# Forgetting attention in key tiles: value products of two tiles in one block, products for the row maxima in the other gap

## The reference

```python
log_f = jax.nn.log_sigmoid((f_logit + b_f).astype(jnp.float32))
Ft = jnp.cumsum(log_f, axis=1).transpose(0, 2, 1)
...
    s = jnp.einsum("bqhd,bkhd->bhqk", qi, k, preferred_element_type=jnp.float32) * scale
    s = s + Fi[..., :, None] - Ft[:, :, None, :]
    ...
    s = jnp.where(kpos[None, :] <= qpos[:, None], s, -jnp.inf)
    p = jax.nn.softmax(s, axis=-1)
    return jnp.einsum("bhqk,bkhd->bqhd", p.astype(v.dtype), v)
```

## Time and profile before

| | |
|---|---|
| median of 3 runs | 3053.46 us |
| span of the profiled execution | 3053.4 us |
| mean granted PE clock over the span | 0.978 |
| PE busy over the span | 2901.2 us, 95% |
| DVE, ACT, POOL busy | 1441.2 us, 1079.7 us, 1064.3 us |
| this attention, layer 1 | from about 1054 to 1292 us of the span |
| this attention, layer 2 | from about 2581 to 2817 us |

### The profile page before, as it was taken

How to read it: one execution, slowest core, us unless ns; L and a number is a source line. 1 busy time by engine, 2 the same in 40 slices (tenths; PEclk the granted TensorE clock), 3 DMA queues, 4 the chain that set the end, 5 groups by cost and what they waited for, 6 DMA issues and landing times. The chain is left out here.

```text
span 3053.4 us, 68189 instructions
## 1 busy us (share of the span) xinstructions
PE 2901.2 (95%) x26644; PEld 2137.6 (70%) x26644; DVE 1441.2 (47%) x2152; ACT 1079.7 (35%) x2188; POOL 1064.3 (35%) x998
## 2 busy tenths in 40 slices
PE   7999989999999899989989999899999998998899
PEld 6867877777777644467768678677777776444677
DVE  5117743323233387767461177432233323877674
ACT  5004433333333234633150044333333332346331
POOL 5101113355555523632151011233555555236221
PEclk9999999999999899999999999999999998999999
DMA  5225543344444341266342255433444443512663
GB/s 159 76 71 166 162 128 95 109 128 131 128 129 128 115 150 40 84 196 205 113 157 76 75 161 161 131 97 109 127 128 132 129 124 115 150 40 84 195 205 114
DMA packets 440642, 383.21 MB, mean 126 GB/s; under 512 B 130696, under 2 KB 369544, under 8 KB 440328
## 3 DMA queue, kind: packets, MB, share of 16 engines
q1 hardware_dynamic: 369576, 345.06, 37.1%
q10 hardware_dynamic: 70752, 33.85, 4.2%
HBM read 239.62 MB, written 139.23 MB: 124 GB/s over the span
## 5 line engine op out<-in xcount | busy, mean ns | idle before, releaser
L147 PE MATMUL ch_acc<-h_hi,ch_w_hi 128*128 128x512 f32 (+1 forms) x2032 | 813.6, 400 | 25.0 <-PEq L144 25.0
L153 PE MATMUL ch_acc<-h_hi,ch_w_lo 128*128 128x512 f32 (+1 forms) x2032 | 821.5, 404 | 0.0
L151 PE MATMUL ch_acc<-h_lo,ch_w_hi 128*128 128x512 f32 (+1 forms) x2032 | 817.7, 402 | 0.0
L147 PEld LDWEIGHTS ch_acc<-h_hi,ch_w_hi 128*128 128x128 f32 (+1 forms) x2032 | 377.6, 186 | 113.0 <-issue 29.1
L151 PEld LDWEIGHTS ch_acc<-h_lo,ch_w_hi 128*128 128x128 f32 (+1 forms) x2032 | 377.1, 186 | 95.9 <-issue 9.8
L153 PEld LDWEIGHTS ch_acc<-h_hi,ch_w_lo 128*128 128x128 f32 (+1 forms) x2032 | 376.9, 185 | 88.0 <-issue 0.3
L115 POOL TENSOR_TENSOR ch_w_lo<-ch_raw,ch_w_hi 128x1024 fp32r<-128x1024 f32 (+1 forms) x62 | 149.8, 2416 | 641.2 <-POOLq L114 641.2
L1814 ACT ACTIVATE fx_prob<-fx_ST 128x512 f32<-128x512 f32 (+3 forms) x320 | 153.9, 531 | 189.6 <-PE fx_ST L1661 95.9
L2069 PE MATMUL so_acc<-ea_wo_hi,so_m_hi 128*128 128x512 f32 x512 | 209.6, 409 | 7.5 <-DVEq L2174 3.8
L2070 PE MATMUL so_acc<-ea_wo_hi,so_m_lo 128*128 128x512 f32 x512 | 204.2, 399 | 0.0
L2071 PE MATMUL so_acc<-ea_wo_lo,so_m_hi 128*128 128x512 f32 x512 | 204.2, 399 | 0.0
(11 more groups left out here) (286 smaller groups left out, 4812.5 us busy)
## 6 DMA issues: line engine op xcount, KB each, us to landing
projT<-ch_stage SPq DMA_DIRECT2D x248, 256.0 KB
ch_raw<-w_in ACTq DMA_DIRECT2D x62, 512.0 KB, 5.4
pj_xb<-x SPq DMA_DIRECT2D x32, 512.0 KB, 4.2
so_stage<-x SPq DMA_DIRECT2D x64, 256.0 KB, 3.0
rp_pre<-projT SPq DMA_DIRECT2D x16, 899.5 KB, 7.6
rs_qx<-projT SPq DMA_DIRECT2D x112, 128.0 KB, 3.3
rs_cs<-rope SPq DMA_DIRECT2D x48, 256.0 KB, 3.6
so_cv<-projT SPq DMA_DIRECT2D x42, 258.0 KB, 3.8
```

Of the source, the lines that this page charges most:

```text
L147: ins = M(acc, self.w_hi[q][:, k, 0:m], self.h_hi[:, k, cols], start=(k == 0), stop=False)
L151: M(acc, self.w_hi[q][:, k, 0:m], self.h_lo[:, k, cols], start=False, stop=False)
L153: ins = M(acc, self.w_lo[q][:, k, 0:m], self.h_hi[:, k, cols], start=False, stop=(k == KC - 1))
```

## The change

Two edits, both in the order of work. On PE, the values of a tile no longer follow the scores of the next tile: they wait until the next even tile, and the values of two tiles stand together behind its scores. In `plan()`, `ahead` is called only behind every second (odd) tile, with the same goals. The number of instructions of every kind is the same.

```diff
@@ plan() @@
-                    goal = int(goal)
-                    ahead(min(total, goal))
+                    if nm % 2 == 0:
+                        ahead(min(total, int(goal)))
@@ PE @@
-            late = None
+            late = []
...
-                    if late is not None:
-                        values(*late)
-                    late = (R, x, nt)
+                    if nt % 2 == 0:
+                        for tile in late:
+                            values(*tile)
+                        late = []
+                    late.append((R, x, nt))
                     nt += 1
                 if k == "o" and R == NR - 1:
-                    values(*late)
+                    for tile in late:
+                        values(*tile)
```

## The result

The changed kernel takes 3066.95 us (median of 5 runs, 3064.34 to 3075.12) against 3053.46 us (5 runs, 3052.82 to 3058.68): ratio 1.0043, 95% interval 1.0031 to 1.0055. It is slower by some 13 us, where 3052.0 with a range of 3039 to 3065 was forecast.

The account below looks back on a forecast made before the run. PE, busy 95% of the span, was taken as the bound, its block distances as the price. Gains of 16.6 less costs of 15.9 leave 0.7 us a layer, 1.4 in both: 3053.4 to 3052.0 us, range 3039 to 3065.

Parts of the forecast that it names:

- gain 1: PE's transitions between kinds of products: a steady pair falls from 5.20 to 4.88 us, 10.6 us gained a layer.
- The rival in which neighbours save nothing: PE's starts stay 1.01 apart between values, other distances keep their average, gain 1 is nil: 3073 us, chance 0.05.
- cost 2: Step `l`: values now ahead of it delay the next round's first scores in seven places, 2.9 us a layer.
- cost 3: Step `u` with ACT's table load, rounds 4 to 6: scores behind it wait 1.02 longer, three times, 3.1 us a layer.
- cost 4: Unfilled gaps on PE: scores following scores in three places, 1.2 us; last term, DVE and POOL lagging, 0.3, a layer.
- gain 2: PE's waits that go, a layer: 4.6 of 5.9 us on reduces, 1.4 of 2.8 on exponentials, together 6.0.
- cost 1: Batches of three maxima products on two buffers: third waits 1.14 in six places, plus 1.23 at `u`, 8.0 us a layer.
- the 8 to 10 forecast: Sign for cost 1: PE's wait on the reduces grows from 5.9 to some 8 to 10 us.
- the add of the even tile stands ahead of the batch's reduces and is held behind POOL: Slower rival, DVE's queue at the batches: first reduce up to 2.2 late, products wait; 3064 us, chance 0.22.
- The prediction's last sign: Outside the two attention stages: the forecast is wrong if anything moves by more than a microsecond.

Follow-up runs that it names:

- e1: The changed kernel with maxima products behind every tile again, as before, so only the values stay in pairs: 3056.68 us, ratio 1.0001.
- f6: e4's kernel with step `l` one tile earlier and the row sums of step `u` ahead of the values: 3040.85 us, ratio 0.9942.
- f10: The kernel before with step `l` one tile earlier and the row sums of `u` ahead of the value product: 3059.34 us, ratio 1.0010.
- f11: f5 and f6 together, with the third maxima product of a batch moved behind the next even tile's values: 3029.50 us, ratio 0.9907.
- e2: The kernel before with maxima products only behind odd tiles, the values of one tile behind each tile's scores as before: 3072.31 us, ratio 1.0053.
- f5: e4's kernel with DVE's eight convolution steps five tiles earlier, ahead of POOL's splitting of `w_out`: 3056.88 us, ratio 1.0002.
- e4: The changed kernel with maxima products behind every tile, as before, in the first three tiles of a layer only: 3063.22 us, ratio 1.0023.
- f8: The kernel before with DVE's convolution steps five tiles earlier and nothing else: 3058.15 us, ratio 1.0001.
- e3: The changed kernel with DVE's reduces ahead of the row sums' add and the convolution step: 3059.98 us, ratio 1.0011.

## Why the prediction was wrong, point by point

**Right: gain 1.** Values to values was taken as 0.91 and is 0.90, values to scores is 0.96 where 1.01 was taken; a steady pair was to be 4.88 instead of 5.20 and is 4.81. The rival in which neighbours save nothing is out. But e1 shows a condition that the prediction did not see: the saving stays only if the second gap is filled.

**Right: costs 2 and 3.** At the first scores of rounds 3 to 7 PE's waits on exponentials in layer 1 rose from 2.0 to 4.2 us in sum (cost 2 took 2.9), at the scores behind the table loads, tiles 60 and 72, from 0.8 to 3.0 (cost 3 took 3.1, with a third place). Behind `u` of round 4 the scores at 1243.74 waited 1.59 (1.3 was forecast, 0.38 before):

```profile
1243.74 0.50 PE L1660 MATMUL fx_ST<-fx_qa,fx_ka 128*128 128x512 f32 x1 [1.59 <-ACT fx_prob L1817]
```

The waits on exponentials rose by 5.1 us in layer 1; costs 2, 3 and 4 without its last term, less the 1.4 of gain 2, were 6.2. What f6 wins in a layer, 10.3, is more than costs 2 and 3 (6.4), but 2.4 of it were to be had without the pairs, by f10.

**Half right: gain 2.** The four waits on reduces behind tiles 8, 10, 16 and 20 of layer 1, 4.7 us of the 5.9, are gone, as forecast. The 1.4 on exponentials is not seen.

**Too high: cost 1.** In layer 1 PE now waits for reduces thirteen times, where it was six. Six of these waits, 5.6 us, are at the batches of three of rounds 1 and 2 (behind tiles 5, 7, 11, 13, 17 and 19), as many places as the forecast priced at 8.0; the one at step `u` is 2.22, where 1.14 and 1.23 were taken. Six more, 4.0 us, are the opening (1.2 before; a seventh batch of three, behind tile 3, is counted here), and one, 4.5, is the stall. So the 14.1 - 4.5 = 9.6 without the stall lie inside the 8 to 10 forecast only because the opening is in them. f11 takes the third product's wait away and rounds 1 to 4 win 2.9 a layer.

**The step that failed** is the last term of cost 4: "Where DVE and POOL both lag, at the start of the second head pair, 0.3." Round 5 lost 6.5 in layer 1 and 6.5 in layer 2, 13 us. The place is wrong too: the second head pair starts with tile 40, where PE waits for no reduce, and the stall is 23 tiles later. The mechanism was among the rivals, as "the add of the even tile stands ahead of the batch's reduces and is held behind POOL", with the price spread over batches in every round (3064, chance 0.22). What happens is the same mechanism in one place a layer, at 4.5 us of wait and a lower clock behind it. It needs two things at once: maxima products in twos (e1 has no such stall, e2 has it) and DVE's convolution steps in the tiles of POOL's splitting of `w_out` (f5 takes it away). That DVE waits at step `u` for ACT's table loads is not shown to be a third: f6 shortens that wait of DVE from 3.40 to 1.83 us, and PE's wait stays 4.4. The prediction set against this rival that 2.4 us lie between adds and batches. That holds only while DVE keeps up, and it looked there and not where DVE and POOL have almost no idle time left, which a row of before shows (9.72 and 9.83 of 10 us).

**What was left out** is the opening. Gain 2 said of the waits there that they stay. Cost 1 counted batches of three in the new list and passed over its run of eight products behind tile 1, their pace and the clock behind them. It cost 2.6 us in layer 1 and 5.8 in layer 2 by the profiled executions (the two differ in the kernel before, 19.0 and 16.1, and not in the changed one, 21.6 and 21.8); in the kernels with maxima products behind each of the first tiles round 0 takes 16.1 to 19.0 in a layer, in those with the new one 20.4 to 22.1, and e4's runs give 6 us for both layers.

The account for both layers: rounds 1 to 4 -7.6, round 5 +13.0, round 0 +8.4, rounds 6 and 7 +2.8, together +16.6 in the stage of this execution, whose span is 18.3 longer; 1.7 lies ahead of and behind the counted tiles. Round 5 and round 0 apart, a layer gained 2.4 us, where the prediction's sum without the 0.3 had 1.0: in sum the other terms were no worse than forecast, with cost 1 too high and gain 2 half there. By the medians the loss is 13.5. Part of the profiled execution's excess over the median (3073.45 to 3066.95) is not explained; the changed kernel's runs spread over 11 us. The prediction's last sign, that nothing outside the two stages moves by more than a microsecond, can't decide: the first scores of layer 1 come 1.3 us later than before, but in f8, which changes nothing ahead of tile 49, they come 6.4 later.

Open: the clock's part of the stall is an estimate. The wait is in the trace (4.48 and 4.47 us in the two layers), but no run held the clock up while PE waited.

## What to carry to other kernels

Before moving work of the bounding engine into larger batches, find the stretch in which the engine that serves it has no idle time left, and price the batch there: an average over the stage hides a single place that costs more than all gains. Here changing who stands first in that queue gave back a part and made another engine wait (e3, round 5 from 76.7 to 71.5); taking other work out of the stretch gave back more (f5, to 66.4). Steps on which a long chain hangs (here `l` and `u`) go ahead of a block that has been made longer, and here that move was worth something only together with the longer block.

## What the runs showed of the hardware

The wait of PE in round 5 cost twice: behind 4.48 us of it the granted clock was 0.50 (1.2 GHz) from 1257.4 to 1263.1, and two tiles' values took 2.92 instead of 1.94. At the low level PE's work behind the wait is late as well.

An add on DVE that starts 0.20 behind one on POOL takes 3.27 and ends 1.09 behind it, near its 1.23 alone; the reduce at 1247.79, which reads PSUM, takes its usual 1.22 while POOL's splitting (1247.55, 2.57) runs. The Trainium skill's "SBUF — State Buffer" (section "SBUF: two separate sides") calls the ports that VectorE and GpSimd share an exclusive lock, held for a whole instruction, where VectorE reads two operands in SBUF and the GpSimd instruction reads SBUF too; these rows agree. At this place the times of DVE's add and of POOL's add ahead of it add up, and the reduces behind the add inherit the sum.
